# Two attention stages worked on pairs of heads or maps, with PSUM banks fixed by use

## The reference

```
# first attention (16 heads, keys 64 wide after folding w_uk into the latent)
logits = q . k * scale + rel_bias[bucket(dist)]      # causal, and only the 256 best keys
p = softmax(logits);  out = p @ v                    # by blocks of 128 queries
# second: MLA (8 heads, 96 wide), difference maps (4 heads, 2 maps each, 32 wide), memory (4 heads, 256 keys)
sc = q @ k.T * scale (causal);  p = softmax(sc);  o = p @ v        # MLA and memory
a = softmax(sc0) - lam * softmax(sc1);  o = a @ v                  # difference maps
```

## Time and profile before

| what | us |
|---|---|
| three runs, median (lowest to highest) | 3574.91 (3573.5 to 3575.41) |
| the profiled execution | 3577.13 |
| its span | 3575.2 |
| PE busy | 3283.7 (92%) |
| DVE busy | 1841.7 (52%) |
| ACT busy | 971.4 (27%) |
| POOL busy | 901.1 (25%) |
| mean granted TensorE clock | 0.943 |

### The profile page before, as it was taken

The page is one execution under the profiler, slowest core; times in us unless marked ns, Lnnn a source line. Parts: engine busy times, 40 slices in busy tenths (PEclk is TensorE's granted clock), DMA queues, the critical chain, the costliest instruction groups (busy, mean ns, idle before and its releaser), DMA issues.

```text
span 3575.2 us, 36793 instructions
## 1 busy us (share of the span) xinstructions
PE 3283.7 (92%) x14026; PEld 2485.9 (70%) x14026; DVE 1841.7 (52%) x3008; ACT 971.4 (27%) x1810; POOL 901.1 (25%) x566
## 2 busy tenths in 40 slices
PE   7999999878779998989999999998997998899898
PEld 4577788555557886668887788887866886555467
DVE  1599991566664447871331544443334326756551
ACT  2420111355552003560001100001214114654340
POOL 0132332000002324653332433332233352100002
PEclk9899999898989999999999999999998999998679
DMA  8012332100001110112332111112112110000012
GB/s 207 12 48 66 91 103 93 60 18 8 17 18 42 48 41 34 44 48 95 102 133 89 36 52 49 47 48 100 61 53 78 48 47 15 1 1 12 0 50 81
DMA packets 185861, 196.37 MB, mean 55 GB/s; under 512 B 12257, under 2 KB 152029, under 8 KB 184029
## 3 DMA queue, kind: packets, MB, share of 16 engines
q1 hardware_dynamic: 170669, 142.08, 13.6%
q10 hardware_dynamic: 15024, 51.98, 3.9%
HBM read 153.15 MB, written 40.89 MB: 54 GB/s over the span
## 4 chain that ended last, share of the span: by engine, by line
PE 69%; DVE 9%; issue 9%; ACT 4%; POOL 4%; DMA 2%; DVEq 2%; POOLq 1%; ACTq 1%; SPq 0%
PE psum L625 66%; PE psum L629 3%; DVE arena L1681 3%; DVE arena L1684 2%; DVE rounded L1681 1%; ACT arena L1292 1%; POOL stat L1166 1%; POOL arena L1220 1%; DVE arena L1832 1%; DMA arena<-z_d 1%; POOL rounded L1177 1%; ACT arena L1402 1%; POOL arena L1237 1%; DVE arena L2207 1%; ACTq L1298 0%
## 5 line engine op out<-in xcount | busy, mean ns | idle before, releaser
L625 PE MATMUL psum<-rounded,rounded 128*128 128x512 f32 (+2 forms) x9504 | 2200.6, 392 | 85.1 <-DVE rounded L1681 44.8
L625 PEld LDWEIGHTS psum<-rounded,rounded 128*128 128x128 f32 x9504 | 1799.7, 191 | 458.0 <-issue 89.0
L625 PE MATMUL psum<-arena 128*128 128x512 f32 (+15 forms) x2450 | 778.9, 494 | 38.3 <-ACT arena L1292 15.5
L1175 POOL CAST rounded<-arena 128x1024 fp32r<-128x1024 f32 (+1 forms) x190 | 205.9, 1084 | 1738.2 <-DMA arena<-in_w_in 826.3
L625 PEld LDWEIGHTS psum<-arena 128*128 128x128 f32 (+4 forms) x2450 | 408.2, 205 | 334.2 <-issue 269.1
L1292 ACT ACTIVATE arena<-psum 128x512 f32<-128x512 f32 (+9 forms) x572 | 307.2, 566 | 754.4 <-PE psum L625 707.3
L1177 POOL TENSOR_TENSOR rounded<-arena,rounded 128x1024 fp32r<-128x1024 f32 (+1 forms) x190 | 466.6, 2456 | 28.2 <-issue 1.3
L629 PE MATMUL psum<-ident,arena 128*128 128x128 f32 (+1 forms) x1816 | 303.6, 313 | 150.4 <-ACT arena L1292 48.7
L629 PEld LDWEIGHTS psum<-ident,arena 128*128 128x128 f32 (+1 forms) x1816 | 242.6, 159 | 239.9 <-issue 92.0
L1681 DVE TENSOR_TENSOR arena<-arena,psum 128x512 f32<-128x512 f32 (+1 forms) x176 | 125.8, 733 | 355.2 <-PE psum L625 335.4
L1681 DVE TENSOR_TENSOR rounded<-arena,rounded 128x1024 fp32r<-128x1024 f32 (+1 forms) x132 | 198.2, 1532 | 210.8 <-ACT rounded L1295 210.2
(11 more groups left out here) (137 smaller groups left out, 1505.0 us busy)
## 6 DMA issues: line engine op xcount, KB each, us to landing
arena<-in_w_in SPq DMA_DIRECT2D x84, 512.0 KB, 3.8
arena<-in_w_ffn_up SPq DMA_DIRECT2D x44, 512.0 KB, 3.8
arena<-in_w_ffn_down SPq DMA_DIRECT2D x22, 512.0 KB, 3.6
z_d<-arena ACTq DMA_DIRECT2D x32, 256.0 KB, 3.0
gate_d<-arena ACTq DMA_DIRECT2D x16, 512.0 KB, 3.9
arena<-in_w_ssm_out SPq DMA_DIRECT2D x16, 512.0 KB, 4.0
arena<-z_d SPq DMA_DIRECT2D x8, 1024.0 KB, 4.8
arena<-gate_d ACTq DMA_DIRECT2D x16, 512.0 KB, 3.3
```

The source lines that it names most:

```text
L625: return pe.matmul(out, lhsT, rhs, start=start, stop=stop)
L1175: pool.tensor_copy(high_part, raw)
```

## The change

Units become pairs: two neighbouring heads of the same block (first attention, MLA, memory), or the two maps of a head (difference maps).

- First attention: keys of all heads are projected once ahead of the loop (`kT`, float32); scores are float32 products over 64 rows, the two heads on the two halves of the rows, issued in turn. The doubling, the splits and the fp32r stacks go. The bias is loaded pair by pair by ScalarE's queue.
- V products: every head has its own 64 stationary columns and its own half of the output rows; the products of the two heads are issued in turn, for 256 queries at a time instead of 512.
- Banks: scores of a pair take banks 0 to 3 (all four from five key blocks on, else two in turn), transposes 4 to 6 in turn, V products bank 7.
- Order: in the first attention and from the difference maps on, TensorE does transposes, V products, then scores; in MLA scores first. ScalarE does the copies ahead of the exponentials. VectorE scales unit s-1 ahead of the masked copies of s; the second head's scaling goes to GpSimd in the first attention and the memory heads, and a scaling by lambda in the difference maps, whose sum then stands at the end of the step, for unit s-2.
- GpSimd's splits of w_x and of the output weights move: one before the last pair, the rest behind the loop.

```diff
-        def bank(name, n=1):
+        def bank(name, n=1, place=None):
-            b = turn[0] if turn[0] + n <= 8 else 0
+            b = place if place is not None else turn[0] if turn[0] + n <= 8 else 0
...
+        probs1 = [[at(off, S) for off in offs] for offs in ((24, 25), (26, 27), (28, 32.5))]
...
+                units1.append(dict(
+                    i=i, nk=i + 1, j=j, q=[qT[64 * m:64 * m + 64, j, i * P:(i + 1) * P] for m in range(2)],
+                    k=[kT[64 * m:64 * m + 64, j, :] for m in range(2)],
...
+        T_LAG1, PV_LAG1 = 3, 4
+        summed_at1 = {n + PV_LAG1: n for n, u in enumerate(units1) if u["i"] % 2}
+        split_at1 = {TT * j + TT - 1 + PV_LAG1 + 5: j for j in range(KT - 1)}
+        def scores_bank(n):
+            return (0, 4) if units1[n]["nk"] > 4 else (2 * (n % 2), 2)
+        def lag2(n):
+            return 2 if n < N_MLA else 3
...
 TensorE, first attention
+            for j in range(8):
+                for half in range(2):
+                    mm(out, ukT[:, j * P:(j + 1) * P], ckvT[:, half * 512:half * 512 + 512]).then_inc(full(("kT", j, half)), 1)
...
             for s in range(STEPS1):
+                if 0 <= s - T_LAG1 < N1:
+                    n = s - T_LAG1
+                    for m in range(2):
+                        pe.wait_ge(odd_ready if m else even_ready, n + 1)
+                        for grp in range(last_group(u) + 1):
+                            four(("T", n, m, grp), [...], 4 + turns % 3)
+                            turns += 1
+                if s in summed_at1:
+                    n = summed_at1[s]
+                    pe.wait_ge(*written(("T", n, 1, last_group(u))))
+                    out = bank(name, 1, 7)
+                    pe.wait_ge(*vacated(name))
+                    for b in range(u["nk"]):
+                        lo = P if b == u["i"] else 0
+                        for m in range(2):
+                            last = mm(out[64 * m:64 * m + 64, lo:256], v[:, u["j"], b * P + 64 * m:b * P + 64 * m + 64],
+                                      at(pT1_at(u, m, b) + lo / Kf, 256 - lo), b == 0, b == u["i"])
                 if s < N1:
+                    place, n = scores_bank(s)
+                    bank(name, n, place)
+                    for k in range(n):
+                        pe.wait_ge(*vacated(name, k))
                     for lo, hi in chunks(u["nk"] * P):
-                        mm(out[:, lo:hi], u["q"], k_high, True, False)
-                        last = mm(out[:, lo:hi], u["q"], k_low, False, True)
+                        for m in range(2):
+                            last = mm(out[:, m, lo:hi], u["q"][m], u["k"][m][:, lo:hi])
...
 TensorE, second attention
             for s in range(STEPS2):
+                if s < N_MLA:
+                    scores2(s)
                 if s in turned_at:
+                    for m in u["lanes"]:
+                        pe.wait_ge(probs2_ready, turned_probs[n] - len(u["lanes"]) + u["lanes"].index(m) + 1)
+                        for grp in range(last_group(u) + 1):
+                            four(("T2", n, m, grp), [...], 4 + turns % 3)
                 if s in summed_at:
+                    out = bank(name, 1, 7)
+                if N_MLA <= s < N2:
+                    scores2(s)
...
 GpSimd
+            for n in range(N1):
+                if n == N1 - TT:
+                    split_weights(("x", 0))
+                pool.wait_ge(sum_inverted, n + 1)
+                pool.tensor_scalar(p, p, rinv[:, c % 8:c % 8 + 1], None, ALU.mult).then_inc(odd_ready, 1)
-            split_weights(*[("x", j) for j in range(3, XT)])
+            split_weights(*[("x", j) for j in range(1, XT)])
...
+            for n in range(N_MLA, N2):
+                if u["ph"] == "d":
+                    pool.tensor_scalar(p1, p1, rinv[:, c % 8 + 1:c % 8 + 2], lam[:, 4:5], ALU.mult, ALU.mult).then_inc(second_scaled, 1)
+            power(("sub", 1))
             split_weights(*[(("o2", 0), k) for k in (0, 2)])
-            power(("sub", 0), ("sub", 1))
...
 ScalarE, first attention (the second in the same order)
             for s in range(STEPS1):
+                if 0 <= s - T_LAG1 < N1:
+                    for m in range(2):
+                        for grp in range(last_group(u) + 1):
+                            copy(at(pT1_at(u, m, 4 * grp), 4, 256)[:, 0:w, here], ("T", n, m, grp), ...)
                 if s < N1:
+                    for m in range(2):
+                        p = probs1[s % 3][m][:, 0:w]
+                        act.activation(p, p, ACT.Exp, scale=-1.0, bias=negmax[:, c % 4:c % 4 + 1],
+                                       accum_out=rsum[:, c % 8:c % 8 + 1]).then_inc(exp_ready, 1)
                 if s - 1 in summed_at1:
+                    copy(attT[:, u["j"], ...], name, psum_of(name)[:, 0:256])
                 if s in split_at1:
...
 VectorE, first attention
             for s in range(STEPS1):
                 if s < N1:
+                    tt_(out[:, :, lo:w], out[:, :, lo:w], bias_pair[u["j"] % 2][:, :, 256 - (w - lo):256], ALU.subtract)
+                if 1 <= s <= N1:
+                    dve.wait_ge(exp_ready, c + 2)
+                    dve.reciprocal(rinv[:, c % 8:c % 8 + 2], rsum[:, c % 8:c % 8 + 2]).then_inc(sum_inverted, 1)
+                    dve.tensor_scalar(p, p, rinv[:, c % 8:c % 8 + 1], None, ALU.mult).then_inc(even_ready, 1)
+                if s < N1:
+                    for m in range(2):
+                        if s >= 3:
+                            dve.wait_ge(*completed(("T", s - 3, m, last_group(units1[s - 3]))))
+                        ins = dve.tensor_tensor_reduce(...)
+                        ins.then_inc(maximum1 if m == 0 else empty(name), 1)
...
 VectorE, second attention: at the end of the step
+                if 2 <= s <= N2 + 1 and units2[s - 2]["ph"] == "d":
+                    dve.wait_ge(second_scaled, n - N_MLA + 1)
+                    stt(p1, p0, rinv[:, c % 8:c % 8 + 1], p1, ALU.mult, ALU.add).then_inc(probs2_ready, 1)
```

More of the change, by code:

```diff
@@ L1 @@
+import itertools
 import math
@@ L389, in hybrid_two_blocks @@
         dtmp = [at(25 + 0.25 * n, TT * SSMH) for n in range(4)]
[L391 to L402, removed]
+        probs1 = [[at(off, S) for off in offs] for offs in ((24, 25), (26, 27), (28, 32.5))]
+        pT1 = [[33.5 + 1.5 * m for m in range(2)], [36.5 + 2 * m for m in range(2)]]
         hBhi, hBlo = [[rounded(off + k) for k in range(KT)] for off in (8, 0)]
@@ L629, in tr, with four @@
                 return pe.transpose(out, src, ident[0:n, 0:n])
-            def four(name, blocks):
-                out = bank(name)
+            def four(name, blocks, place=None):
+                out = bank(name, 1, place)
                 pe.wait_ge(*vacated(name))
@@ L1055, in _ @@
                 if s in summed_at:
                     n = summed_at[s]
[L1057 to L1066 removed]
+                    u, name = units2[n], summed(n)
@@ new lines, in _ @@
+                    pe.wait_ge(*written(("T2", n, 1, last_group(u))))
+                    out = bank(name, 1, 7)
+                    pe.wait_ge(*vacated(name))
+                    for b in range(u["nk"]):
+                        lo = P if b == u["i"] and u["ph"] != "e" else 0
+                        for m in range(2):
+                            last = mm(out[64 * m:64 * m + 64, lo:256], u["v"](m, b), at(pT2_at(u, m, b) + lo / Kf, 256 - lo),
+                                      b == 0, b == u["nk"] - 1)
@@ new lines, in _ @@
+                    if same_area(n) is not None:
+                        act.wait_ge(*completed(same_area(n)))
+                    here = slice((u["i"] % 2) * P, (u["i"] % 2 + 1) * P)
+                    for m in u["lanes"]:
+                        for grp in range(last_group(u) + 1):
+                            name = ("T2", n, m, grp)
+                            if u["ph"] == "e":
+                                copy(at(pT2_at(u, m, 0), 512), name)
+                                continue
+                            w = min(4, u["nk"] - 4 * grp)
+                            copy(at(pT2_at(u, m, 4 * grp), 4, 256)[:, 0:w, here], name,
+                                 psum_of(name)[:, 0:w * P].rearrange("p (a b) -> p a b", b=P))
@@ new lines, in _ @@
+                if s < N2:
+                    u, name = units2[s], ("S2", s)
+                    w = u["nk"] * P
+                    dve.wait_ge(*completed(name))
+                    if u["ph"] == "e":
+                        dve.tensor_reduce(negmax4[s % 3], psum_of(name).rearrange("p (a b) -> p a b", b=MEMT),
+                                          axis=AX.X, op=ALU.min).then_inc(maximum2, 1)
+                    else:
+                        held = held_by(s)
+                        for m in range(2):
+                            c = 2 * s + m
+                            if held is not None and (u["ph"] == "m" or m == 1):
```

(6 more changed lines are left out.)

517 lines of the change are left out of this document (233 added, 284 removed).

## The result

| what | us |
|---|---|
| after, four runs, median (lowest to highest) | 3690.26 (3688.87 to 3692.15) |
| before, four runs beside them, median | 3574.73 |
| ratio after to before, 95% interval | 1.0324 [1.0306, 1.0342] |
| span of the profiled execution, after (before) | 3688.5 (3575.2) |
| mean granted TensorE clock, after (before) | 0.914 (0.943) |

The account below looks back on a forecast made before the run. No engine is full in the first attention, where PE stands behind ACT's tail; MLA is PE-bound. 3577 + 63 - 10 + 15 - 3 + 3 = 3645, less 2, plus 3 for shape changes: 3646 us, range 3590 to 3770.

Parts of the forecast that it names:

- (a): From five blocks on, a pair's scores fill all four score banks, so they start only when DVE ends step s-1.
- (b): First attention: with 5 to 8 blocks the fourth transpose group waits for ACT's first copy, queued behind exponentials of s-1.
- (c): First attention: one V bank, copied last in ACT's even step, so odd steps' V products and the scores behind them wait.
- First attention, +63 forecast: First attention grows from 448.6 to 512 us: 459 at full clock plus 53 for clock 0.75; bounds +28 to +169.
- The table of steps: First attention, time between DVE's ends for i = 0 to 7 at full clock, sum 52 us a pair, 416 for eight.
- 159/3 = 53 more: First attention: 159 us of PE work at full clock takes 53 us more at a granted clock of 0.75.
- Difference maps, +15 forecast: Maps take 176 us against 161, the weighted sum and its transposes standing ahead of the next scores; -8 to +21.
- MLA, -10 forecast: MLA: V products halve, 36.1 us a pair against 38.6, half the saving given back to wait (a); 0 to -15.
- -3 and +3 forecast: Memory heads -3 us from shorter units and half V; +3 us for two w_out_2 splits now last on POOL.
- R2: Clock holds at 0.90 in the first attention, maps stay at 161: 3596 to 3610 us; chance 0.12.
- R1: Column halves don't overlap, so V products cost 7.7 us a pair more at full clock: 3746 us; chance 0.20.
- R3: First attention: (b) and (c) don't bind as PE lets scores pass waiting V products; stage 312, kernel 3440 to 3510; chance 0.13.

Follow-up runs that it names:

- V products head by head: Changed kernel with first-attention V products issued all blocks of one head, then the other, instead of in turn: 3748.67 us, 1.0496 to the kernel before.
- twelve fillers: Changed kernel plus twelve 128x128 float32 products without use behind each first-attention step's scores: 3640.93 us, 1.0192 to the kernel before.

## Why the prediction was right, and what in it was mis-sized

- **The mechanism.** Waits (a), (b) and (c) were all found, each in its steps. DVE waits 280 us for scores (over 150 was forecast), PE 99.6 + 45.6 us for ACT's copies (over 100). Taking (c) away gave 50 us back, tightening (b) cost 27.5, and taking both out of the scores' way turned the loss of 87 us into a gain of some 75.
- **First attention, +63 forecast, +87 measured.** The table of steps had the right shape (4.7, 7.0, 5.1, 8.3, 4.5, 7.0, 5.5, 9.9 at full clock; 5.3, 9.9, 5.3, 10.2, 4.9, 9.4, 6.9, 12.4 measured) and the stage's clock was 0.75 as forecast, but a pair takes 64.2 us, over the 52 to 60 named as a sign. The forecast was 300 us of other work and hand-overs, 159 of PE at full clock and "159/3 = 53 more" for the clock. Over the chain of waits of the stage the trace has 263, 185 and 85: PE is on the chain for 270 us, and the granted clock over these pieces is 0.69. Two things in PE's part were too small. Its work is 26 us dearer than the table, and its clock on the chain is below the stage's mean, which also counts time when PE isn't on the chain. The 37 us too many in the other terms hid part of it. PE's V products and scores at i = 3 show both: 4.05 us in the table, 4.52 at a granted clock of 1.00 (twelve fillers, from 794.26), 6.18 at 0.73 (from 871.26). The lower bound (28) and the upper (169) held.
- **Difference maps, +15 forecast, +24 measured.** The forecast's 176 us stood on 161 for before; between the same events before is 172.2 and after 196.4, so the stage came out 20 us over the forecast. The chain (two masked copies, sum, transposes, scores) is the one forecast. The failure is the choice of 176, below the 182 of the forecast's own 0.68, "with the clock low partly where PE is not late". PE was late where the clock was low: 0.61 in the stage, 0.59 over PE's pieces of the chain. The forecast's sum at that clock, 91 + 62/0.61 = 193, comes near the 196, but in part by luck: the chain has 126 us of PE, 75 at full clock instead of 62, and 70 of the rest instead of 91.
- **MLA, -10 forecast, +4.1 measured.** This term had the wrong sign. PE is no longer full: between the same events it is busy 136.8 of 161.6 us, where it was 150.0 of 157.5. But a pair of heads was forecast at 36.1 us against 38.6 of PE's work before. Over the last three pairs, between the ends of masked copies, it takes 40.8 against 41.7, and the first pair up to its last masked copy takes 6.6 us longer. The gain of 7.7 us a pair that the forecast counted for the V products is nearly all given back. By the forecast's own figures (30.9 of PE's work, period 36.1) two thirds would have been, not half. PE waits 23.2 us for DVE's masked copies by wait (a) and the clock is 0.94 instead of 0.98; how the rest divides no run tells.
- **Memory heads and the rest.** -3 and +3 forecast, -1.0 and +1.3 measured. These are too small for the windows to tell apart, and no run shows the 3 for changes of shape.
- **The total.** The second attention and what follows were forecast at +5, and measured +28.7 (4.1, 24.3, -1.0 and 1.3). The total is 44 us over the forecast and stays in range since that is 180 us wide, from R2's lower end to past R1.
- **R1 (column halves don't overlap, 3746)** is refuted by V products head by head. The total lies between forecast and R1, but for another reason. The Trainium skill ("TensorE: Matmul & The Clock Gate", Part 3) gives a gain of 2.38 for three products on separate column groups of 32; for two halves of 64, issued in turn, this case shows two passes in the time of one.
- **R2 (the clock holds)** is refuted by 0.75 and 0.61. **R3 (faster)** had its mechanism turned round: PE's queue does not let scores pass a V product that waits, but the order of calls can, and then the first attention takes 371 us. R3's own 312 was too low by 59; it counted DVE and wait (a) alone, and DVE still waits 111 us for scores.

## What to carry to other kernels

On an in-order queue, issue first what the next engine in the relay needs, and put behind it whatever waits for a copy-out: here the same work took 533 or 371 us by that alone. A buffer freed by the last instruction of another engine's step costs not that instruction but everything queued behind the wait. Where PE's passes lie on a chain that leaves it idle between, count them below the stage's mean clock: here 0.69 against 0.75, and 0.59 against 0.61 in the maps, where short passes after a wait ran at 0.50. And before stages of two kernels are compared, both must be cut at the same events.

## Hardware behaviour that was not expected

GpSimd's multiplication by a column took longer than the bound taken from its two-operand operations, and far longer than the same with two multiplications; by shape, first attention (one multiplication):

```profile
L1250 POOL TENSOR_SCALAR arena<-arena,rinv 128x1024 f32<-128x1024 f32 x7 | 23.7, 3382 | 28.8 <-DVE rinv L1884 28.8
```

and the maps (two):

```profile
L1329 POOL TENSOR_SCALAR arena<-arena,rinv,lam 128x1024 f32<-128x1024 f32 x3 | 3.6, 1201 | 25.3 <-DVE rinv L2293 25.3
```

3.38 us against 1.20 for the same 1024 elements, where at most 2.47 was forecast. The memory heads have the form with one multiplication too, and there 256 columns took 0.99 us, against 1.06 in the first attention and 0.56 with two multiplications in the maps: it goes with the form and not with the stage. No run here shows why. It was hidden, with two steps of time. The other surprise is that 732 products without use make a stage 48 us shorter.
